# A delta-rule recurrence in 64x64 diagonal blocks, with three units in flight instead of two

## Time and profile before

| what | value |
|---|---|
| median of three executions | 4665.15 us |
| the profiled execution | 4663.12 us |
| its span, first to last instruction | 4661.4 us |
| mean granted TensorE clock over the span | 0.890 |
| TensorE busy, share of the span | 86% |
| weight loads busy | 78% |
| VectorE busy | 55% |
| ScalarE busy | 36% |
| DMA over the span | 122 GB/s |
| the recurrence | 2817 to 3746 us |

### The profile page before, as it was taken

One profiled execution on the slowest core, in us unless ns is written; L12 is line 12 of the kernel. 1 busy time (PEld: TensorE's weight loads), 2 busy tenths in 40 slices (PEclk: granted clock), 3 DMA queues, 4 the chain that ended last, 5 costly groups with the idle time before them and its releaser, 6 DMA issues.

```text
span 4661.4 us, 78517 instructions
## 1 busy us (share of the span) xinstructions
PE 4030.5 (86%) x29468; PEld 3621.7 (78%) x29468; DVE 2571.5 (55%) x4265; ACT 1670.2 (36%) x2326; POOL 23.7 (1%) x46
## 2 busy tenths in 40 slices
PE   7999777577999999998799646888888898999998
PEld 6999333355999999998689545776677788999998
DVE  3744776444647777544434335666766645444443
ACT  3545333212435555433213232222222135555433
POOL 0000000000000000000000000000000000000000
PEclk9999667666999999999899777888888889999999
DMA  4554666112444555554124000000000043555553
GB/s 159 180 187 176 230 232 264 59 51 89 175 163 153 181 183 185 171 181 153 63 99 144 34 0 11 3 2 2 2 2 2 1 168 142 185 181 180 172 183 123
DMA packets 80486, 568.08 MB, mean 122 GB/s; under 512 B 9472, under 2 KB 9728, under 8 KB 15520
## 3 DMA queue, kind: packets, MB, share of 16 engines
q1 hardware_dynamic: 78048, 558.50, 33.8%
q0 software_dynamic: 2368, 8.65, 0.5%
HBM read 565.02 MB, written 2.10 MB: 122 GB/s over the span
## 4 chain that ended last, share of the span: by engine, by line
PE 77%; DVE 13%; issue 5%; ACT 3%; DMA 1%; DVEq 1%; ACTq 0%; POOL 0%; SPq 0%; POOLq 0%
PE po L256 17%; PE po L257 17%; PE po L258 17%; PE po L1135 5%; PE pa L738 2%; PE po L814 2%; PE po L443 2%; PE pa L814 1%; PE pa L302 1%; PE po L738 1%; PE pa L1457 1%; PE po L1218 1%; DVE hf L313 1%; PE po L1226 1%; DVE j_work L852 0%
## 5 line engine op out<-in xcount | busy, mean ns | idle before, releaser
L244 DVE TENSOR_TENSOR w_lo<-raw,w_hi 128x1024 fp32r<-128x1024 f32 x880 | 1039.2, 1202 | 604.8 <-ACT w_hi L237 586.9
L256 PE MATMUL po<-hh,w_lo 128*128 128x256 f32 x4256 | 1207.0, 284 | 24.3 <-DVE hh L337 12.6
L257 PE MATMUL po<-hh,w_hi 128*128 128x256 f32 x4256 | 1206.4, 283 | 0.0
L258 PE MATMUL po<-hh,w_hi 128*128 128x256 f32 x4256 | 1206.3, 283 | 0.0
L237 ACT ACTIVATE w_hi<-raw 128x1024 fp32r<-128x1024 f32 (+1 forms) x877 | 898.4, 1038 | 804.4 <-PE po L258 621.6
L256 PEld LDWEIGHTS po<-hh,w_lo 128*128 128x128 f32 x4256 | 819.2, 192 | 25.6 <-issue 25.5
L257 PEld LDWEIGHTS po<-hh,w_hi 128*128 128x128 f32 x4256 | 819.3, 193 | 0.0
L258 PEld LDWEIGHTS po<-hh,w_hi 128*128 128x128 f32 x4256 | 819.1, 192 | 0.0
L256 PE MATMUL po<-f_hi,w_lo 128*128 128x256 f32 x1408 | 400.0, 284 | 6.2 <-DVE f_lo L1315 6.2
L257 PE MATMUL po<-f_lo,w_hi 128*128 128x256 f32 x1408 | 399.9, 284 | 0.0
L258 PE MATMUL po<-f_hi,w_hi 128*128 128x256 f32 x1408 | 399.8, 284 | 0.0
(11 more groups left out here) (539 smaller groups left out, 6501.3 us busy)
## 6 DMA issues: line engine op xcount, KB each, us to landing
raw<-ffn_up SPq DMA_DIRECT2D x176, 1024.0 KB, 4.8
raw<-w_in SPq DMA_DIRECT2D x112, 1024.0 KB, 4.8
raw<-ffn_down SPq DMA_DIRECT2D x64, 1024.0 KB, 4.9
raw<-ada SPq DMA_DIRECT2D x56, 1024.0 KB, 4.8
ada_buf<-ada SPq DMA_DIRECT2D x40, 1024.0 KB, 6.2
raw<-w_out SPq DMA_DIRECT2D x32, 1024.0 KB, 4.8
raw<-ffn_down SPq DMA_DIRECT2D x32, 768.0 KB, 4.2
raw<-glu SPq DMA_DIRECT2D x16, 1024.0 KB, 4.8
```

The source lines that it names most:

```text
L244: dve.tensor_tensor(w_lo[:, k % 4, 0:width], raw[:, k // 2, (k % 2) * PW:(k % 2) * PW + width], w_hi[:, k % 4, 0:width].bitcast(F32), ALU. ...
L256: pe.matmul(po[bank][:, 0:T], lo, act_hi[:, t, :], start=first and n == 0, stop=False)
L257: pe.matmul(po[bank][:, 0:T], hi, act_lo[:, t, :], start=False, stop=False)
L258: mm = pe.matmul(po[bank][:, 0:T], hi, act_hi[:, t, :], start=False, stop=end)
```

## The change

Every chunk matrix is kept as its two diagonal blocks side by side: [128, 4, 64], the first block in rows 0 to 63, the second in rows 64 to 127. All products with them are 64x64: `heads` (tiles in all four quarters of the array, two halves per name), `blocks_pe` for the inversion (a first half in the tiles (0,0) for one direction and (1,1) for the other, then, behind a wait on `j_half`, the second half with the tiles swapped), and `nv` likewise. Masks and transposes on VectorE work on 256 columns where they had 512 and on 128 where they had 256; the masks are loaded as 11 of 64 columns instead of 10 of 128. The inversion becomes a stream of its own with banks of its own (one a direction, pa[3] and po[3]), so that three units are in flight: the chunk of one, the inversion of the next and the preparation of the one after it. `PERIOD` replaces the 18 stages: V is a piece of the inversion, C of the chunk, P of the preparation, O of post. `ab` and `ak` now follow one another on the banks of `im`; post uses the chunk's banks. Preparation waits for the keys (`kk`) of the unit before instead of its `nv1`.

```diff
--- before
+++ after
+        def narrow(bank, first=0):
+            return bank[:, first:first + 4 * C].rearrange("p (m s) -> p m s", m=4)
+
+        def all4(mask):
+            return k_masks[:, mask:mask + 1, :].broadcast_to([P, 4, C])
+
+        def blocks_pe(pe, n, sets, k, outs, lhs, rhs):
+
+            for swap in range(2):
+                if swap:
+                    pe.wait_ge(j_half, n * 10 + k)
+                settle(pe)
+                mm = [None, None]
+                for m in range(4):
+                    for e in range(2):
+                        r = half(e ^ swap)
+                        w = rhs[e][r, m, :]
+                        o = outs[e][r, m * C:m * C + C]
+                        if w.shape[1] < C:
+                            o, w = o.rearrange("p (a s) -> p a s", a=2), w.unsqueeze(1).broadcast_to([C, 2, C // 2])
+                        mm[e] = pe.matmul(o, lhs[e][r, m, :], w, start=True, stop=True)
+                if swap == 0:
+                    mm[1].then_inc(j_half, 1)
+            for e in range(2):
+                mm[e].then_inc(sets[e][0], 1)
...
-                each_of(pe, b[0], i_a, i_t).then_inc(by_pe, 1)
+            blocks_pe(pe, n, sets, 2 * l - 1, [s[3][0] for s in sets], [s[2][0] for s in sets], [s[2][1] for s in sets])
...
+            lhs = [i_p if l == 5 and want == "tt" else i_tt for _, _, (i_a, i_t, i_tt, i_p), b, want in sets]
+            rhs = [i_tt if l == 5 and want == "tt" else i_p[:, :, 0:C // 2] for _, _, (i_a, i_t, i_tt, i_p), b, want in sets]
+            blocks_pe(pe, n, sets, 2 * l, [s[3][1] for s in sets], lhs, rhs)
...
-                dve.tensor_tensor(i_tt, i_a, over(masks[:, 0:1, :], i_p), ALU.mult).then_inc(by_dve, 1)
+                dve.tensor_tensor(i_tt, i_a, all4(0), ALU.mult).then_inc(by_dve, 1)
...
                 else:
-                    dve.tensor_tensor(packed(i_p, w), lower(as_wide(b[0], i_p), w), lower(m, w), ALU.mult)\
+                    dve.tensor_tensor(packed(i_p, w), lower(narrow(b[0]), w), lower(m, w), ALU.mult)\
                        .then_inc(by_dve, 1)
...
-        j_a, k_nt, j_p = pair("j_a", [4, P], H0, 2), pair("k_nt", [4, P], H0 + 4, 2), pair("j_p", [4, P], H0 + 8, 2)
-        j_work = pair("j_work", [4, P], H0 + 12, 2)
-        j_inv = {x: pair(f"j_inv_{x}", [4, P], H0 + 16 + 4 * n, 2) for n, x in enumerate("cl")}
+        j_a, j_p = pair("j_a", [4, C], H0 + 12, 1), pair("j_p", [4, C], H0 + 14, 1)
+        j_work, k_nt = pair("j_work", [4, C], H0 + 16, 1), pair("k_nt", [4, C], H0 + 18, 1)
+        j_inv = {x: pair(f"j_inv_{x}", [4, C], H0 + 20 + 2 * n, 1) for n, x in enumerate("cl")}
...
-        k_masks = sb("k_masks", [10, P], R3)
+        k_masks = sb("k_masks", [11, C], R3)
...
-        CHUNK_POINTS = (0, 1, 2, 3, 4, 5, 6, 7, 9, 11, 13, 15)
+        PERIOD = "V C V C C V C V C C V C V C C V C V C P C V P O V P O V P O P O P O P P P".split()
...
-        X, I, M = (pa[2], po[2]), (pa[0], pa[1], po[0], po[1]), (pa[3], po[3])
...
+        X, I, inv_bank = (pa[2], po[2]), (pa[0], po[0], pa[1], po[1]), (pa[3], po[3])
+
+        j_half = sem("jinv_half")
         j_done = [(sem(f"jinv_pe{e}"), sem(f"jinv_dve{e}")) for e in range(2)]
-        jinv = {x: [j_done[0] + ((j_a[0][:], j_work[0][:], j_inv[x][0][:], j_p[0][:]), (I[0], I[1]), "tt"),
-                    j_done[1] + ((j_a[1][:], j_inv[x][1][:], j_work[1][:], j_p[1][:]), (I[2], I[3]), "t")] for x in "cl"}
+        jinv = {x: [j_done[0] + ((j_a[0][:], j_work[0][:], j_inv[x][0][:], j_p[0][:]), (inv_bank[0], inv_bank[0]), "tt"),
+                    j_done[1] + ((j_a[1][:], j_inv[x][1][:], j_work[1][:], j_p[1][:]), (inv_bank[1], inv_bank[1]), "t")] for x in "cl"}
...
-        def woven(prep, chunk, post=None):
-            def step(stream):
+        def woven(**streams):
+
+            for turn in PERIOD:
+                stream = streams.get(turn)
                 if stream is not None:
                     next(stream, None)
-            for stage in range(18):
-                if stage in (0, 2, 3, 4, 6):
-                    step(post)
...
-        def phases(eng, prep, chunk, post):
-
-            woven(prep(eng, 0, "c"), None)
-            woven(prep(eng, 0, "l"), chunk(eng, 0, "c", False))
+
+        def phases(eng, prep, inverse, chunk, post):
+
+            woven(P=prep(eng, 0, "c"))
+            woven(V=inverse(eng, 0, "c"), P=prep(eng, 0, "l"))
             with eng.Fori(0, 7) as j:
-                woven(prep(eng, j + 1, "c"), chunk(eng, j, "l"))
-                woven(prep(eng, j + 1, "l"), chunk(eng, j + 1, "c"), post(eng, j))
-            woven(None, chunk(eng, 7, "l"))
-            woven(None, None, post(eng, 7))
+                woven(C=chunk(eng, j, "c"), V=inverse(eng, j, "l"), P=prep(eng, j + 1, "c"))
+                woven(C=chunk(eng, j, "l"), V=inverse(eng, j + 1, "c"), P=prep(eng, j + 1, "l"), O=post(eng, j))
+            woven(C=chunk(eng, 7, "c"), V=inverse(eng, 7, "l"))
+            woven(C=chunk(eng, 7, "l"), O=post(eng, 7))
...
             pe.wait_ge(k_up_in, j * 16 + 16)
             if x == "l":
-                pe.wait_ge(*pre_a["c"].at(j, "nv1"))
+                pe.wait_ge(*pre_v["c"].at(j, "kk"))
             elif not first_unit(j, x):
-                pe.wait_ge(*pre_a["l"].at(j - 1, "nv1"))
+                pe.wait_ge(*pre_v["l"].at(j - 1, "kk"))
...
-                    pe.matmul(M[e][:, n * T:n * T + T], k_w[half(e), n, :], zl[half(e), n, H], start=True, stop=True)\
+                    pe.matmul(I[e][:, n * T:n * T + T], k_w[half(e), n, :], zl[half(e), n, H], start=True, stop=True)\
...
+            def here(v, a, n, r):
+                o = n * P + r * C + (off(x) if any(v is w for w in k_ah) else 0)
+                return v[half(a), o:o + C]
+
+            def heads(swap, bank, w, m):
+                settle(pe)
+                for n in range(2):
+                    for r in range(2):
+                        mm = []
+                        for e in range(2):
+                            a = e ^ swap
+                            o = (2 * a + n) * C
+                            mm.append(pe.matmul(bank[e][half(r), o:o + C], here(w[e], a, n, r), here(m[e], a, n, r),
+                                                start=True, stop=True))
+                return mm
+
+            pe.wait_ge(*V.at(j, "ah1"))
+            pe.wait_ge(*A.at(j, "a1"))
+            heads(0, I[0:2], (k_bh[0], k_ah[1]), (k_ah[0], k_bh[1]))
             pe.wait_ge(*A.at(j, "bk1"))
...
+            heads(0, I[2:4], k_kh, k_ah)[1].then_inc(Q.did("hd"), 1)
+            yield
+            pe.wait_ge(*Q.at(j, "hd"))
+            for e, mm in enumerate(heads(1, I[0:2], (k_bh[0], k_ah[1]), (k_ah[0], k_bh[1]))):
+                mm.then_inc(Q.did(f"im{e}"), 1)
+            for e, mm in enumerate(heads(1, I[2:4], k_kh, k_ah)):
+                mm.then_inc(Q.did(f"nt{e}"), 1)
+            yield
+            pe.wait_ge(*V.at(j, "nt1"))
+            for swap in range(2):
+                if swap:
+                    pe.wait_ge(*Q.at(j, "hv"))
+                settle(pe)
                 for a in range(2):
                     for n in range(2):
-                        o = n * P + 64 * a
-                        mm = pe.matmul(M[e][:, o:o + 64], k_nt[e][:, 2 * a + n, :],
-                                       k_vt[:, n + (2 if x == "l" else 0), half(a)], start=True, stop=True)
-                mm.then_inc(Q.did(f"nv{e}"), 1)
+                        mm = []
+                        for e in range(2):
+                            r, o = half(e ^ swap), n * P + 64 * a
+                            mm.append(pe.matmul(I[2 + e][r, o:o + 64], k_nt[e][r, 2 * a + n, :],
+                                                k_vt[r, n + (2 if x == "l" else 0), half(a)], start=True, stop=True))
+                if swap == 0:
+                    mm[1].then_inc(Q.did("hv"), 1)
+            for e in range(2):
+                mm[e].then_inc(Q.did(f"nv{e}"), 1)
+            if x == "l":
+                pe.wait_ge(*V.at(j, "rh1"))
+                heads(0, I[0:2], k_bh, k_rh)[1].then_inc(Q.did("bh"), 1)
+                pe.wait_ge(*Q.at(j, "bh"))
+                for e, mm in enumerate(heads(1, I[0:2], k_bh, k_rh)):
+                    mm.then_inc(Q.did(f"ab{e}"), 1)
+            yield
+            if x == "l":
+                pe.wait_ge(*V.at(j, "ab1"))
+                heads(0, I[0:2], k_kh, k_rh)[1].then_inc(Q.did("kh"), 1)
+                pe.wait_ge(*Q.at(j, "kh"))
+                for e, mm in enumerate(heads(1, I[0:2], k_kh, k_rh)):
+                    mm.then_inc(Q.did(f"ak{e}"), 1)
...
-            pe.matmul(I[1][:, 0:T], k_bd[:], k_nrm[:], start=True, stop=True).then_inc(Q.did("sum"), 1)
+            pe.wait_ge(*A.at(j, "nv0"))
+            pe.matmul(I[2][:, 0:T], k_bd[:], k_nrm[:], start=True, stop=True).then_inc(Q.did("sum"), 1)
...
-            yield
-            yield
-            pe.wait_ge(*V.at(j, "ak1" if x == "l" else "eps"))
-            settle(pe)
```

(49 more changed lines are left out.)

137 lines of the change are left out of this document (41 added, 96 removed).

## The result

The kernel after takes 4729.2 us (median of 4 runs, 4717.6 to 4731.5) where the kernel before, run beside it, takes 4665.4 (4664.6 to 4667.7): ratio 1.0131, 95% interval 1.0113 to 1.0148. The profiled execution is 4731.52 us with a span of 4729.9; before it was 4663.12. It is slower, as forecast: by 64 us in the medians and 68 in the profiled executions, where 97 were forecast.

A forecast was written before the change was run, and what follows sets the result against it. TensorE and VectorE in a chain, neither full, bound the recurrence. Seven bodies 875 (130 less 5 each), prologue 76 and epilogue 79 make 1030 against 929 us: +100, rounded to 97, so about 4762 us; range 4715 to 4820.

The forecast's parts named there:

- The mechanism: In the recurrence, 64x64 products lose TensorE's 2.4 GHz level; granted clock 0.5 to 0.6 where it was 0.81; chance 0.70.
- One reason that the forecast gave for the low level: Earlier trace: products using 8 rows of the array, busy 3.40 of 3.40 us, yet run at clock 0.50.
- One product: TensorE, one inversion product: two halves of 8 slots with 0.34 us between, 2.05 us low, 1.22 high, against 1.78.
- VectorE: Halved operands save 0.14 us per 128 columns, 0.28 per 256, some 18 us a head; share about 45%.
- Rounds and tails: Body rounds: latent 10.9 us, context 7.1 low, 6.9 and 4.6 high; low-clock tails: context 21.4, latent 28.8.
- the sum of a body: One loop body at the low clock: context half 53.7 plus latent half 76.3, together 130 us.
- the 5 that I had taken: Taken off the body's 130 us for short stretches at clock 1.00, leaving 125 against 112.6.
- Half of it: Rival: context rounds at the high clock, latent ones low; 118 us a head, about 4715 us; chance 0.08.
- The clock stays high: Rival: rounds keep the 2.4 GHz level; 97.5 us a head, 4552 us for the kernel; chance 0.18.
- No overlap: Rival: the two tiles of a half run one behind the other, 1.71 us more each step, near 5000; chance 0.02.
- the last line: Chances for the kernel's time: faster by more than about 0.2% 0.20, within 0.04, slower by more 0.76.
- the 0.65 taken: Head products, preparation: half of a name costs 0.65 us at the low clock, the middle of 0.43 to 0.86.

The follow-up runs named there:

- run 4: Kernel after with the order of the kernel before (two units in flight), 64x64 tiles kept: 4729.7 us, ratio to before 1.0156.
- run 11: Kernel after, bodies written out, 8+8 full-array fillers ahead of each inversion, one behind each `u` of latent chunks: 4608.2 us, ratio to before 0.9875.
- run 3: Kernel after with full-array fillers ahead of inversions and in rounds, plus four in each of four preparation places, two with an added wait: 4737.3 us.
- run 10: Kernel after, looped, with the longer full-array filler bursts ahead of inversions (8+16 and 8+8) but none inside the rounds: 4675.3 us, ratio to before 1.0026.
- run 9: Kernel after, bodies written out, 8+8 full-array fillers ahead of each inversion, one behind each `ks` and `u` of latent chunks: 4619.4 us, ratio to before 0.9912.
- runs 1 to 3, 6 and 10: Kernel after plus, in 1, full-array fillers: 4660.9 us; in 2, the same on one 64x64 tile: 4808.7; in 6, longer full-array bursts, looped: 4628.3.
- run 8: Kernel before with full-array fillers in its preparation: 4675.0 us, ratio to before 1.0024.
- runs 4 and 12: 12: kernel after with the old order and 64x64 tiles, plus 8+8 fillers ahead of each inversion and two behind each inversion product: 4645.9 us.

## Why the prediction was right

**The mechanism holds.** The clock of the stage fell to 0.60 as forecast. Full-array products in the waits turn +1.3% into 0.0% where small ones of the same length in the same places make it +3.2%, and longer bursts of them give -0.7% (looped). The loss comes with the tiles and not with the order (run 4).

One reason that the forecast gave for the low level was weaker than it looked. The 8-row products of the earlier trace rows were part of a busy stretch that began at 1001.12, and full 128x128 products behind them in the same stretch have the low level too:

```profile
1007.00:1011.00 4.00, 4.00 (x20) 3.76 (x19) 3.88 (x10) 0.00 (x0) 0.00 (x0) 0.50 0.00 0
```

So that row doesn't tell small products from full ones. The two kinds of filler do, and the latent rounds, busy 30.19 of 32 us at 0.50, fit them.

**One product.** 2.14 us at the low level (2.05 forecast), the hand-over 0.38 beyond a slot (0.34). At the high level it is 1.34 (1.22).

**VectorE.** Its steps shrank by 0.13 (0.42 to 0.29) and 0.27 (0.70 to 0.43) us, its share of the stage is 49% (45% forecast), and in the rounds its adds wait for TensorE all the same.

**Rounds and tails.** Latent 10.7 us (10.9), context 7.6 low and 5.15 high (7.1, 4.6); latent at the high level, with fillers, 6.9 to 7.0 (6.9). Added again from its own terms, the high-level rounds of the forecast are 7.0 and 4.7, not 6.9 and 4.6. Context tail 20.8 us (21.4), from the add at 3155.61 to the end of L1642 at 3176.37; latent tail 27.1 to 29.8 (28.8).

**The step that was off is the sum of a body.** It was 130 us at the low clock level. The fourth body's rounds ran wholly low (its context half is 3249.57 to 3301.89, its latent half from there to 3375.59; only stretches of the tails were at 1.00): 52.3+73.7 = 126.0. The context half is 1.4 under its 53.7. In the latent half the opening and the four rounds took 44.1 us where 47.5 stood. The last latent chunk writes no state, so its `d` has no products for one, and I had charged the full `d` of 4.8 us. In this body's last latent chunk L1705 and L1706 don't run, and `pa`'s L1709 starts at 3341.28 without them. The timeline of TensorE in an ordinary chunk shows what they take, up to the start of L1709:

```profile
3203.44 0.79 PE L1705 MATMUL pa<-k_u,k_bk 64*128 64x128 f32 x2 [0.30 <-ACT k_u L1724]
3204.03 0.63 PE L1706 MATMUL pa<-k_vt,k_bk 64*128 64x128 f32 x2
3204.59 0.69 PE L1709 MATMUL pa<-k_rh,k_S 128*128 128x64 f32 x2
```

1.15 us a direction, 2.3 of the 3.4. The tail was 27.1 for 28.8. Against these stands the loop's return, 2.6 us, which I had left out: 130-1.4-3.4-1.7+2.6 = 126. The mean body is 121.0, since in the other bodies some rounds ran high: 5.0 us less, the 5 that I had taken. That these two agree is in part luck, for I had looked for the short stretches in the preparation, and they came mostly in the context rounds. Prologue and epilogue came out at 74.0 and 77.3 us (76, 79). Seven bodies at 4 us less, 3.7 from the ends: 32 of 1030, less the 3 by which I rounded down.

**The rivals.** *Half of it* was true of the context rounds of four bodies, in which the level rose within the second round (5.9, 5.2, 5.4 us for the second to fourth), and of two more from the third round on; it was priced at 4715: the truth lies between it and the forecast, which had a chance for it of only 0.08. *The clock stays high*, 4552, was the right question, and no run had the level throughout. With it held in the latent rounds (run 11) the body is 104.8 us, not 97.5: the context opening and rounds take 25.5 us on average where 21.5 stood, the latent ones 29.4 (30.7), and the tails 20.6 and 29.4 (19.3 and 26). The tails of that run are mostly low, as this latent one shows:

```profile
3058.90:3088.20 29.30, 21.21 (x259) 16.34 (x260) 21.31 (x51) 8.81 (x19) 1.07 (x2) 0.60 0.03 11
```

Where fillers brought them to the high level (run 3) they took 19.3 and about 27 us, near the forecast. *No overlap* falls by the first two rows of the step above. Four tiles abreast cost less than I took, see below. The chances of the cases that are slower (low clock, half, no overlap) add up to 0.80, where the last line has 0.76.

## What to carry to other kernels

Before cutting products to the size of their data, ask what the granted clock of the stretch hangs on: here small tiles saved work on two engines and lost the clock of the one that the chain waits for. Test such a loss with fillers of the same length, once on the whole array and once on a small tile; if only the full ones help, it is the clock, and a few full-array products in waits that stand anyway can give it back. Their place has to be tried: run 3 put in more of them and lost it all. Look at a loop's return as a term of its own, and read every special case of a loop (a last chunk without state) before multiplying.

## What the runs showed that was not expected

Four 64x64 tiles do run four abreast. The head products of the kernel after, at the low clock level: the first group of four and the next record, then the first record of a later half and of the half behind it:

```profile
3165.13 0.37 PE L1474 MATMUL pa<-k_ah,k_bh 64*64 64x64 f32 x1
3165.14 0.37 PE L1474 MATMUL po<-k_bh,k_ah 64*64 64x64 f32 x1
3165.15 0.37 PE L1474 MATMUL pa<-k_ah,k_bh 64*64 64x64 f32 x1
3165.16 0.37 PE L1474 MATMUL po<-k_bh,k_ah 64*64 64x64 f32 x1
3165.30 0.31 PE L1474 MATMUL pa<-k_ah,k_bh 64*64 64x64 f32 x1
...
3166.86 0.34 PE L1474 MATMUL pa<-k_ah,k_bh 64*64 64x64 f32 x1 [0.17 <-PE po L1474]
...
3167.31 0.31 PE L1474 MATMUL pa<-k_ah,k_kh 64*64 64x64 f32 x1
```

A half of a name is four slots, 0.45 us, near the 0.43 that was the lower bound and not the 0.65 taken.

The level depends on more than the work at hand. In the kernel after, all loop bodies open their context half alike (9.42 us to the first add, at the low level), yet the level rose in the second round in four of them, later in two, and not at all in one, so that the same rounds took 5.15 us or 7.6. Behind a burst (run 10) the second and third of them took 5.12 to 5.16 in all seven; in run 9 some that began high fell back to 8.5. And in run 10 one latent half kept 6.8 us where the others went to 10.7. What decides it was not found. Kernels with a moving clock also spread more: 4654.4 to 4686.9 us for run 10, against 4654.6 to 4666.4 for the kernel before, run beside it.

The loop's return costs VectorE 2.53 to 2.83 us in every looped kernel of the new order (after, runs 1 to 3, 6 and 10), and the profile calls it "issue", so a theory built on waits doesn't see it. It is no fixed price of a loop: in the kernel before, with fillers (run 8) or without, and in the tiles with the old order (runs 4 and 12) VectorE's timeline lists no idle time of that kind. In run 4 TensorE has it instead, 2.76 to 3.74 us ahead of the first product of a body (L1443, six times); in the kernel before neither of the two has any at that place. What makes the difference was not tested.
